# A ring of four one-bank GEMM results, and position biases added by VectorE

## What is computed

```python
# swa (block 1); moba adds bias_c[t5_bucket(own_diff)] in the same way
diff = qi[:, None] + L - sj[None, :]
bias = bias_a[t5_bucket(diff)].astype(jnp.float32).transpose(2, 0, 1).reshape(SWA_KV_HEADS, grp, L, 2 * L)
s = jnp.where(valid[None, :, None, None], s + bias, NEG_INF)

# differential attention (block 2), one head has two maps m and one bias
rel = q_pos[:, None] - k_pos[None, :]
bias = rel_bias.astype(jnp.float32)[t5_bucket_2(rel)]
logits = jnp.einsum('bqhmd,bkhmd->bhmqk', qi, k).astype(jnp.float32) * scale
logits = logits + bias.transpose(2, 0, 1)[None, :, None]
logits = jnp.where((rel >= 0)[None, None, None], logits, NEG_INF_2)
p = jax.nn.softmax(logits, axis=-1)
p = p[:, :, 0] - lam_full * p[:, :, 1]
...
# pooling branch: a window mean of each channel group, a 256x256 product per group
# (pool_w), a scale, and an output product (pool_o)
```

## Time and profile before

| | |
|---|---|
| median of 3 runs | 2458.18 us (2454.41 to 2463.07) |
| the profiled execution | 2459.62 us, of which the span from first to last instruction is 2457.8 |
| PE | busy 2329.1 us, 95% of the span, 17913 matmuls |
| DVE | busy 1697.4 us, 69% |
| ACT | busy 1201.9 us, 49% |
| POOL | busy 87.8 us, 4% |
| chain that ended last | PE 77%, DVE 15%, ACT 5% |
| granted clock of PE | mean 0.967 of 2.4 GHz |
| DMA | 400.89 MB, mean 163 GB/s |

### The profile page before, as it was taken

One profiled execution on the slowest core, in us unless ns is written; L12 is line 12 of the kernel. 1 busy time (PEld: TensorE's weight loads), 2 busy tenths in 40 slices (PEclk: granted clock), 3 DMA queues, 4 the chain that ended last, 5 costly groups with the idle time before them and its releaser, 6 DMA issues.

```text
span 2457.8 us, 43525 instructions
## 1 busy us (share of the span) xinstructions
PE 2329.1 (95%) x17913; PEld 2225.7 (91%) x17913; DVE 1697.4 (69%) x2655; ACT 1201.9 (49%) x1803; POOL 87.8 (4%) x78
## 2 busy tenths in 40 slices
PE   6998898999999999999999999999999999999997
PEld 5977898999999987889898999999997889898997
DVE  6656887986664897787555664664897787555653
ACT  2565446764444434555535444444434555535443
POOL 1000000110110000000000110110000000000110
PEclk7998999999999999999999999999999999999998
DMA  8634575667656563346444655656553346444662
GB/s 241 189 103 145 161 251 160 200 188 225 182 176 190 172 179 95 112 129 189 145 139 137 181 182 159 182 176 188 173 180 95 112 130 188 146 139 136 183 184 81
DMA packets 397941, 400.89 MB, mean 163 GB/s; under 512 B 18006, under 2 KB 391112, under 8 KB 397745
## 3 DMA queue, kind: packets, MB, share of 16 engines
q1 hardware_dynamic: 395361, 389.27, 52.1%
q0 software_dynamic: 2384, 8.85, 1.1%
HBM read 396.98 MB, written 1.09 MB: 162 GB/s over the span
## 4 chain that ended last, share of the span: by engine, by line
PE 77%; DVE 15%; ACT 5%; issue 3%; DMA 1%; DVEq 0%; ACTq 0%; POOL 0%; POOLq 0%
PE gemm_ps L866 62%; DVE weights_lo L1475 4%; PE gemm_ps L869 4%; DVE y L1925 3%; PE misc_ps L1017 2%; PE misc_ps L1016 2%; PE misc_ps L951 2%; PE misc_ps L969 1%; DVE mod_partial L1572 1%; ACT weights_hi L1142 1%; ACT e L1273 1%; DVE y L1625 1%; PE misc_ps L1049 1%; PE misc_ps L1034 1%; PE misc_ps L1013 1%
## 5 line engine op out<-in xcount | busy, mean ns | idle before, releaser
L1475 DVE TENSOR_TENSOR weights_lo<-raw_weights,weights_hi 128x1024 fp32r<-128x1024 f32 x704 | 836.5, 1198 | 448.3 <-ACT weights_hi L1142 446.4
L866 PE MATMUL gemm_ps<-h_hi,weights_hi 128*128 128x256 f32 x3536 | 1008.8, 285 | 41.8 <-DVE h_lo L1611 27.6
L1142 ACT CAST weights_hi<-raw_weights 128x1024 fp32r<-128x1024 f32 x704 | 719.0, 1034 | 673.1 <-PE gemm_ps L866 609.5
L866 PE MATMUL gemm_ps<-h_lo,weights_hi 128*128 128x256 f32 x3536 | 995.5, 282 | 0.0
L866 PE MATMUL gemm_ps<-h_hi,weights_lo 128*128 128x256 f32 x3536 | 994.1, 281 | 0.0
L866 PEld LDWEIGHTS gemm_ps<-h_hi,weights_hi 128*128 128x128 f32 x3536 | 673.5, 190 | 50.4 <-issue 46.3
L866 PEld LDWEIGHTS gemm_ps<-h_lo,weights_hi 128*128 128x128 f32 x3536 | 673.1, 190 | 2.9 <-issue 2.2
L866 PEld LDWEIGHTS gemm_ps<-h_hi,weights_lo 128*128 128x128 f32 x3536 | 671.2, 190 | 0.0
L866 PE MATMUL gemm_ps<-hidh,weights_hi 128*128 128x256 f32 x880 | 248.4, 282 | 1.8 <-DVE weights_lo L1475 1.8
L866 PE MATMUL gemm_ps<-hidl,weights_hi 128*128 128x256 f32 x880 | 246.6, 280 | 0.0
L866 PE MATMUL gemm_ps<-hidh,weights_lo 128*128 128x256 f32 x880 | 246.3, 280 | 0.0
(11 more groups left out here) (289 smaller groups left out, 2665.9 us busy)
## 6 DMA issues: line engine op xcount, KB each, us to landing
raw_weights<-in_ffn_w_dram SPq DMA_DIRECT2D x256, 512.0 KB, 3.9
raw_weights<-in_w_in_dram SPq DMA_DIRECT2D x200, 512.0 KB, 3.7
raw_weights<-in_w_mod_dram SPq DMA_DIRECT2D x48, 512.0 KB, 4.9
raw_weights<-in_w_up_dram SPq DMA_DIRECT2D x44, 512.0 KB, 4.6
raw_weights<-in_xattn_kv_dram SPq DMA_DIRECT2D x32, 512.0 KB, 4.4
raw_weights<-in_w_out_dram SPq DMA_DIRECT2D x24, 512.0 KB, 4.5
raw_weights<-in_w_down_dram SPq DMA_DIRECT2D x20, 512.0 KB, 4.5
raw_weights<-in_w_branch_dram SPq DMA_DIRECT2D x16, 512.0 KB, 4.6
```

Of the source, the lines that this page charges most:

```text
L866: mm = pe.matmul(ps[:, c, 0:T], w[:, m, kt, c * P:(c + 1) * P], x[:, f, :], start=start, stop=stop_)
L1142: act.copy(unit_of(WH, m % SPLIT, u), unit_of(RAWB, u["raw"] % RAW, u)).then_inc(sems["weights_rounded"], 1)
L1475: dve.tensor_tensor(unit_of(WL, m % SPLIT, u), unit_of(RAWB, u["raw"] % RAW, u), unit_of(WH, m % SPLIT, u), ALU.subtract).then_inc(sems["w ...
```

## The change

Four things change together.

1. `GP` becomes a ring of RING = 4 results, each with both tiles in one bank of 2 x 256 columns; a GEMM waits for the evacuation of the fourth before it. Since two tiles share a bank, only the first matmul of a result starts and only the last stops an accumulation. The pooling inputs are made as two GEMMs of 256 columns in place of one of 512, with two evacuations.
2. The second matmul of the scores goes, and FLIP with it. DVE adds the bias: it reads PSUM and `hank` and writes E (two instructions a head), takes the maxima of E, and ACT makes the exponentials in place in E. The next head's scores now wait for these additions, not for the exponentials; DVE waits for hank and for the transpose that last read its E.
3. `hank` now must hold the bias in query order without reversal. POOL therefore expands the lines in DRAM by three new transfers (`bias_rows`): each writes 8 x 128 rows of 384 numbers at a pitch of 385, so that a load with a pitch of 384 reads row p shifted by p. `pool_hankel` waits for all three and loads the same amount as before. For moba it loads after the additions of swa's last head.
4. The evacuation of pool_w on DVE waits for both halves of ACT's.

```diff
+ROWS = P * (LINE + 1)
+RING = 4
     add("bias")
+    for i in range(3):
+        add("bias_rows", which=i)
-    moba_in.append(("hankel", dict(which=1, l=0, after=("scores", "swa", 3))))
+    moba_in.append(("hankel", dict(which=1, l=0, after=("biased", "swa", 3))))
             def inputs(j):
-                z2(l, "pool", j, "evac_v2", form="T", cols=2 * COLS, dst="pt", c0=j * COLS)
+                for c in (j, j + 1):
+                    z2(l, "pool", c, "evac_v2", form="T", dst="pt", c0=c * COLS)
-    GP = ctx.enter_context(nc.psum_tensor("gemm_ps", [P, 2, 2, 512], F32))
+    GP = ctx.enter_context(nc.psum_tensor("gemm_ps", [P, RING, 2, COLS], F32))
     def slot(pid):
-        return GP[:, pid % 2, :, 0:T]
+        return GP[:, pid % RING]
-                sp.dma_start(FLIP[:], a["flip"]).then_inc(sems["consts_in"], 16)
-                up("consts_in", by=16)
         def pe_unit(u):
             if u["first"]:
-                if u["pair"] >= 2:
-                    pe.wait_ge(*done(("evac", u["pair"] - 2)))
+                if u["pair"] >= RING:
+                    pe.wait_ge(*done(("evac", u["pair"] - RING)))
...
-                        start = u["first"] and kt == 0 and n == 0
-                        stop_ = u["last"] and kt == u["nkt"] - 1 and n == 2
+                        start = u["first"] and kt == 0 and n == 0 and c == 0
+                        stop_ = u["last"] and kt == u["nkt"] - 1 and n == 2 and c == tiles - 1
         def pe_scores(k):
             if state["scores"] is not None:
-                pe.wait_ge(sems["act_attn"], at("exps", *state["scores"]))
+                if state["scores"][0][:5] == "cross":
+                    pe.wait_ge(sems["act_attn"], at("exps", *state["scores"]))
+                else:
+                    pe.wait_ge(sems["vec_attn"], at("biased", *state["scores"]))
-            if c["hname"] is not None:
-                pe.wait_ge(sems["hankel_in"], at(*c["hname"]))
...
-                        pe.matmul(ps, c["q"][m][:, qt * P:(qt + 1) * P], c["k"][m][:, 0:nk], start=True, stop=False)
-                        mm = pe.matmul(ps, FLIP[:], c["hank"][:, c["head"][m], T - nk:T], start=False, stop=True)
+                        mm = pe.matmul(ps, c["q"][m][:, qt * P:(qt + 1) * P], c["k"][m][:, 0:nk], start=True, stop=True)
         def act_softmax(k):
-                    act.activation(c["E"][:, qt, m, 0:nk], scores_at(c, qt, m, nk), ACT.Exp, bias=NM[:, j:j + 1], accum_out=DEN[:, j:j + 1]).then_inc(sems["act_attn"], 1)
+                    logits = scores_at(c, qt, m, nk) if c["maps"] == 1 else c["E"][:, qt, m, 0:nk]
+                    act.activation(c["E"][:, qt, m, 0:nk], logits, ACT.Exp, bias=NM[:, j:j + 1], accum_out=DEN[:, j:j + 1]).then_inc(sems["act_attn"], 1)
         def vec_softmax(k):
             dve.wait_ge(sems["pe_attn"], at("scores", k["cfg"], k["i"]))
+            if M == 2:
+                dve.wait_ge(sems["hankel_in"], at(*c["hname"]))
+                if c["pack"] == "diff":
+                    if k["i"]:
+                        dve.wait_ge(sems["pe_attn"], at("turned", k["cfg"], k["i"] - 1, 0))
+                elif k["i"] >= 2:
+                    dve.wait_ge(sems["pe_attn"], at("turned", k["cfg"], k["i"] - 2, 1))
+                elif k["cfg"] == "moba":
+                    dve.wait_ge(sems["pe_attn"], at("turned", "swa", k["i"] + 2, 1))
+                biased = []
+                for qt in range(2):
+                    nk = P * (qt + 1)
+                    rows = c["hank"][:, c["head"][0]:c["head"][0] + (1 if c["pack"] == "diff" else 2), T - nk:T]
+                    if c["pack"] == "diff":
+                        rows = rows.to_broadcast([P, 2, nk])
+                    dve.tensor_tensor(c["E"][:, qt, :, 0:nk], PB[:, 0:2, P * qt:P * qt + nk], rows, ALU.add).then_inc(sems["vec_attn"], 1)
+                    biased.append(up("vec_attn", ("biased", k["cfg"], k["i"])))
             for qt in range(2):
...
+                if M == 2:
+                    dve.wait_ge(sems["vec_attn"], biased[qt])
+                dve.tensor_reduce(NM[:, 2 * qt:2 * qt + M], c["E"][:, qt, :, 0:nk] if M == 2 else PB[:, qt, 0:nk], AX_X, ALU.max, negate=True).then_inc(sems["vec_attn"], 1)
         def vec_pool_w(k):
-                dve.wait_ge(sems["act_split"], at("split_hi", "G", f"l{l}mq", f))
+                dve.wait_ge(sems["act_split"], at("split_hi", "G", f"l{l}mq", 2 * g + 1))
+        def pool_bias_rows(k):
+            i = k["which"]
+            pool.wait_ge(sems["line_out"], at("lines_out"))
+            src = bass.AP(tensor=scratch.tensor, offset=i * 8 * LINE, ap=[[LINE, 8], [0, P], [1, LINE]])
+            dst = bass.AP(tensor=scratch.tensor, offset=3 * 8 * LINE + i * 8 * ROWS, ap=[[ROWS, 8], [LINE + 1, P], [1, LINE]])
+            pool.dma_start(dst, src).then_inc(sems["bias_rows"], 16)
+            up("bias_rows", ("bias_rows",), by=16)
         def pool_hankel(k):
-            pool.wait_ge(sems["line_out"], at("lines_out"))
+            pool.wait_ge(sems["bias_rows"], at("bias_rows"))
...
-            src = bass.AP(tensor=scratch.tensor, offset=k["which"] * 8 * LINE, ap=[[1, P], [LINE, 8], [1, T]])
+            src = bass.AP(tensor=scratch.tensor, offset=3 * 8 * LINE + k["which"] * 8 * ROWS + P - 1, ap=[[LINE, P], [ROWS, 8], [1, T]])
```

More of the change, by code:

```diff
@@ L594, in build @@
     CC, SP4, QG = sb("silu_c", [P, NF]), sb("softplus4", [P, NF]), sb("qk_gains", [P, 4])
-    ONES, IDENT, FLIP, HEADS = (sb(n, [P, P]) for n in ("ones", "ident", "flip", "headsum"))
+    ONES, IDENT, HEADS = (sb(n, [P, P]) for n in ("ones", "ident", "headsum"))
     EPS = sb("eps", [P, 4])
@@ L634, in build @@
     n_pairs = 1 + max([k["id"] for kind, k in steps if kind.startswith("evac")], default=-1)
-    last_pairs = [p for p in (n_pairs - 2, n_pairs - 1) if p >= 0]
-    GP = ctx.enter_context(nc.psum_tensor("gemm_ps", [P, 2, 2, 512], F32))
+    last_pairs = range(n_pairs - RING, n_pairs)
+    GP = ctx.enter_context(nc.psum_tensor("gemm_ps", [P, RING, 2, COLS], F32))
     PB = ctx.enter_context(nc.psum_tensor("misc_ps", [P, 4, 512], F32))
@@ L850, in pe_unit @@
             if u["first"]:
-                if u["pair"] >= 2:
-                    pe.wait_ge(*done(("evac", u["pair"] - 2)))
+                if u["pair"] >= RING:
+                    pe.wait_ge(*done(("evac", u["pair"] - RING)))
                 else:
                     pe.wait_ge(sems["vec_setup"], at("x", 0, 3))
-            ps = GP[:, u["pair"] % 2, :, :]
+            ps = slot(u["pair"])
             tiles = u["cols"] // P if u["form"] == "F" else TT
@@ L1261, in act_evac_v1 @@
             act.wait_ge(sems["gemm_done"], at("unit", k["last_unit"]))
-            act.copy(BUF[k["dst"]][:, :, k["c0"]:k["c0"] + k["cols"]], GP[:, k["id"] % 2, :, 0:k["cols"]]).then_inc(sems["act_drain"], 1)
+            act.copy(BUF[k["dst"]][:, :, k["c0"]:k["c0"] + k["cols"]], slot(k["id"])[:, :, 0:k["cols"]]).then_inc(sems["act_drain"], 1)
             up("act_drain", ("evac", k["id"]))
@@ L1672, in vec_v2 @@
             for t in range(TT):
-                dve.tensor_scalar(BUF[k["dst"]][:, t, k["c0"]:k["c0"] + k["cols"]], GP[:, k["id"] % 2, t, 0:k["cols"]], RT[:, t:t + 1], None, ALU.mult).then_inc(sems["vec_drain"], 1)
+                dve.tensor_scalar(BUF[k["dst"]][:, t, k["c0"]:k["c0"] + k["cols"]], slot(k["id"])[:, t, 0:k["cols"]], RT[:, t:t + 1], None, ALU.mult).then_inc(sems["vec_drain"], 1)
                 up("vec_drain", ("evac", k["id"]))
@@ L2008, in pool_bias @@
             pool.wait_ge(sems["act_setup"], at("lines_read"))
-            pool.dma_start(scratch.rearrange("i h j -> h i j"), o_set["lines"][:]).then_inc(sems["line_out"], 16)
+            lines = bass.AP(tensor=scratch.tensor, offset=0, ap=[[LINE, 8], [8 * LINE, 3], [1, LINE]])
+            pool.dma_start(lines, o_set["lines"][:]).then_inc(sems["line_out"], 16)
             up("line_out", ("lines_out",), by=16)
+        def pool_bias_rows(k):
[5 more added lines that the diff above has]
+            up("bias_rows", ("bias_rows",), by=16)
         def pool_hankel(k):
-            pool.wait_ge(sems["line_out"], at("lines_out"))
+            pool.wait_ge(sems["bias_rows"], at("bias_rows"))
             pool.wait_ge(sems["vec_setup"], at("setup_end"))
@@ L2050, in pool_mem_load @@
             up("mem_in", ("memt", k["l"]), by=16)
-        parts = dict(setup=pool_setup, bias=pool_bias, hankel=pool_hankel, mem_load=pool_mem_load, hid_split=pool_hid_split, pads1=pool_blocks)
+        parts = dict(setup=pool_setup, bias=pool_bias, bias_rows=pool_bias_rows, hankel=pool_hankel, mem_load=pool_mem_load, hid_split=pool_hid_split, pads1=pool_blocks)
         for kind, k in steps:
@@ L2091, in shape_constants @@
     windows = np.ascontiguousarray(np.stack(windows, axis=1).astype(np.float32))
-    return {"ident": np.eye(P, dtype=np.float32), "flip": np.ascontiguousarray(np.eye(P, dtype=np.float32)[::-1]),
```

(4 more changed lines are left out.)

3 lines of the change are left out of this document (1 added, 2 removed).

## The result

The changed kernel takes 2463.89 us (median of 20 runs, 2458.59 to 2468.12), the kernel before 2456.57 (20 runs, 2451.50 to 2463.07). The ratio is 1.0028, 95% interval 1.0020 to 1.0036: about 7 us slower, where 15 us faster was predicted. The profiled execution has a span of 2462.0 us against 2457.8.

What follows compares the result with a forecast made beforehand. PE was read as 95% busy, with DVE close and the next limit in block 2's attention. From 2459.62 us, -10 (block 2) - 8 - 1 (block 1) + 4 (start) = -15 gave 2444.6 us, range 2430 to 2465.

Steps and rivals of the forecast that it cites:

- attention of block 2: Both layers' attention stages: faster PE limited by DVE's work and waits, 5 us gained per layer, 10 us in all.
- block 1: Attention of block 1: 8 us gained at 140 to 230 us (bounds 3 to 14), 1 us at 230 to 330.
- start: Start of the kernel: three DRAM copies delay hank, gate-block and weight loads, 4 us lost, bounds 0 and 31.
- Rivals 1 and 2: Start, PE waiting at L1075: first, rows land late, 2471.6 us, chance 0.13; second, half the engines, 2452.6 us, chance 0.15.
- rival 2: Start: each copy on 8 of 16 engines, landing at 88, 8 us wait plus 4 of weights, 2452.6 us; chance 0.15.
- over 93%: Sign that the forecast is right: DVE over 93% busy at the attention of block 2.
- Score blocks: PE's score matmuls per head: 1.5 us instead of 3.90, bounds 0.66 and 1.95 us.
- The ring: GEMM result banks: nothing won in feed-forward; PE's 4.32 us pool_w stop, twice, already counted in block 2's waits.
- the split that comes with the ring: Pool inputs in block 2: eight evacuations of 256 columns instead of four of 512 cost DVE 0.6 us per layer.
- DVE's wait for the transposed head before: DVE's softmax work writing E: this wait costs nothing while the transpose is some us ahead of the softmax.

Runs made afterwards that it cites:

- rows32: Changed kernel with 32 skewed copies of each bias line instead of 128 (384 KB per set), read by four loads of 32 partitions: 2448.77 us.
- block2_only: rows32 with DVE's additions in block 2 alone; in block 1 PE adds the bias rows by an identity matmul: 2449.22 us.
- runs 1 and 2: First: rows32, 2448.77 us. Second: kernel before plus only the three 1536 KB copies, which nobody reads and the hank load waits for: 2472.18 us.
- run 3: Also late_rows: changed kernel with the second and third copies issued behind the gate blocks, first hank load waiting for the first copy alone: 2464.31 us.
- ring_only: The change without its bias part: kernel before with the ring of four and eight pool results of 256 columns, bias still a PE matmul: 2464.15 us.
- nobias_ring: Kernel before with the bias matmul left out, nothing added in its place, and the ring of four results of one bank: 2423.19 us.
- ring_wide: rows32 with pool results of 512 columns, each taking two neighbouring banks of the ring, so no split: 2451.69 us.

## Why the prediction was wrong, step by step

The sum was -10 (attention of block 2) - 9 (block 1) + 4 (start) = -15. Without the copies the kernel gains 9 (rows32, 6 to 13 by its interval), and the copies cost 15: -9 + 15 = +6, against 7 measured. So of the 22 us between forecast and result 11 are the start's. The other 10 or so are the -19 of the other terms, of which -9 was measured, and block2_only points to the -9 of block 1 as what was too much.

- **The start, +4 taken, 14 to 15 measured** (runs 1 and 2). This is the term that turned the sign. The time of the copies came out near: they had landed at 80.8 us (forecast 78), the gate blocks at 94.7 (forecast 90). That is in part luck, since the price took the pace of the hank load, which has up to 16 packets in flight, and a copy has half of that (next point). The step that failed stands in the same paragraph: "a second stream on the engines delays the next loads" was seen, with ACT's margin of 0.60 us, and then given 4 us. The row that was wanted is the DMA share ahead of the stage, 1.07 at 60 to 75 us. With the engines full the loads had to wait for the 4608 KB of copies, and half of the copies' own time is what that came to. By bytes at the rate of that row (338 GB/s) they would be an estimated 14 us, which fits the three together, but not the single copy of run 3, which cost next to nothing. The bounds (0 to 31) held it by luck: 28 of the 31 us were a stop at L1075 that didn't come.
- **Rivals 1 and 2** put the loss at L1075, behind late gate blocks. That matmul waited for nothing of its own; the slower outcome came by the weights. By the rule of the Trainium skill (DMA: Bandwidth & Descriptors, section on why a DMA increments its semaphore by 16) each copy runs on 8 engines, and the packets of the traces agree. While the first copy of run 3 is alone (49 to 60 us), it has 7 or 8 packets in flight for most of the time and more than 8 for under 0.2 us in all; in the changed kernel the copies have some 15 in flight from 53 to 61 us and 6 to 9 from 63 to 77. So rival 2 had the engines right, two copies beside each other and the third behind; its landing (88), its place of the loss (L1075) and its 12 us were not.
- **Attention of block 2, -10 taken, -5.1 twice in the trace.** Right in size. Additions at 678 and 415 ns, rows as foreseen (682 and 415). DVE as the next limit, most of rstd_q gone, gh gone: right. DVE is 88% busy instead of over 93%: its 154.67 us and its waits of 19.7 make 174.4 of 175, so it has no spare time, but that was so before too (142.22 and 32.1 of waits): its waits were filled with work, and the sign of over 93% was set too high.
- **Score blocks, 1.5 us taken, 0.86 measured.** The lower bound, two maps side by side (0.66), was the nearer one. The Trainium skill (TensorE: Matmul & The Clock Gate, Part 3 on packing small matmuls) says that matmuls on separate rows of the array run at the same time; the block of 0.86 us agrees, being shorter than the 1.3 us of its four durations one after the other (an estimate from the earlier trace rows, whose matmuls have 128 rows). The error of 0.6 us a head cost the forecast nothing, since the gain of PE ran into DVE anyway.
- **Block 1, -9 taken.** The traces give -4.7 (after) and -3.8 (rows32) from n = 481 to 1700, where the second trace of before has -1.7. Its first part, 121 to 240 us, regained the 8 us of the forecast. The second part lost 3.3 where 1 us of gain was taken: the bound of 4 was the right end. DVE, at 83.2 of 100 us, had no room for 4.2 us more. Block2_only shows that the additions of block 1 as a whole are worth nothing that can be told, so the term of 9 us fails with them.
- **The ring, nothing of its own.** Right: no gain in the feed-forward, and the stop at pool_w is gone and given back a little later. In ring_only it comes back at a score block, and in the changed kernel as the 4.4 us for `gl` (L1966) in the list above: DVE's evacuation of that pool_w result stands behind a softmax there as well, and the product that reads gl waits for it. But the split that comes with the ring was priced by its 0.6 us of DVE per layer, while alone it costs 6 us in the kernel before: in a stretch where DVE is full, PE's stop was 0.9 us longer and a fall of its clock followed.
- **DVE's wait for the transposed head before**: no row names it, as taken.

What stays open: where the last 2 us of the split go, and why the whole gain of rows32 is 9 us by the medians and 14.8 between two traces. Of these, 2.8 us lie between the two traces of before, and the profiled execution of rows32 was its fastest, 2444.4 of a median of 2448.8.

## What to carry to other kernels

Price a new transfer by what is queued with it, above all if the DMA share of its stretch is near 1 and the consumer's margin is under a microsecond. Here three copies at once cost 15 of their 33.7 us, and moving two of them by 20 us didn't help; one of 1536 KB by itself, or three of 384 KB, cost next to nothing. That is one kernel's share and no rule. Ask first how little data does the same: here a quarter of the copies turned a loss of 0.3% into a gain of 0.4%. When work moves from a full engine to one that is at 80 to 90% in the same stage, price both sides by a run that leaves the work out and one that does it twice: here PE's microsecond was worth 0.5 and DVE's cost 1.0 to 1.1, so moving 3.04 us against 1.09 per head gained little.

## What the runs showed of the hardware

GEMM matmuls of 256 columns that follow one another without a stop at a granted clock of 1.00 start either every 113.3 or every 117.8 ns, for stretches of up to some 130 us. Busy times of 20 us of feed-forward in the first and then the second trace of the kernel before, in which PE has no gap:

```profile
460.00:480.00 20.00, 20.00 (x179) 20.00 (x178) 18.55 (x26) 15.87 (x24) 2.97 (x2) 1.00 0.61 191
```

```profile
460.00:480.00 20.00, 20.00 (x172) 20.00 (x171) 17.70 (x26) 13.98 (x23) 1.50 (x1) 1.00 0.57 176
```

179 against 172 matmuls (the clock's column is the 1.00). Over nearly all of the 120 us behind 400 us, the first trace of before and those of nobias_ring, ring_wide and late_rows were at the faster step, the other ten at the slower one, so two traces can differ by 4.2 us there with nothing changed. What sets the level isn't known. Whoever explains a few microseconds by two traces should take a second trace of the same kernel first.

A stop of PE of 0.40 us left the granted clock at 1.00 and one of 1.26 us at the same place was followed by a mean of 0.83 over 20 us. At that place of the first layer, though, a stop of 0.42 us was followed by the fall in one trace of the kernel before and not in the other, so its length alone doesn't decide.

A copy from DRAM to DRAM of 1536 KB, of size 8 in its slowest dimension, had about 8 packets in flight when alone, two beside each other about 15. From the issue to the next load on POOL's queue it took 15.1 us beside the weight stream, three issued at once 33.7 us.
